# Two transformer blocks on one core: the memory's first key unit moved in front of the first MLP

## The reference, cut to what matters

```
x  = x + gate1 * (merged @ w_out)
h2 = rmsnorm(x, g_norm2) * (1 + scale2) + shift2
x  = x + gate2 * (square(relu(h2 @ w_mlp1)) @ w_mlp2)
x  = rmsnorm(x, g_final)
...
mem_n = rmsnorm(mem, mem_norm)                # over the 1024 features
h  = rmsnorm(x, norm_mix[0])
proj = h @ a_w_in[0]                          # gates, conv input, qm
kv = mem_n @ w_mem_kv[0]                      # k: columns 0:256, v: columns 256:512
k  = rmsnorm(k per head of 64, k_gain)        # the key's own norm
q  = rmsnorm(qm per head of 64, q_gain)
o  = softmax(q k^T / 8) v
```

## Time and profile before

| | |
|---|---|
| time, median of 3 runs | 1140.02 us (1136.89 to 1140.96) |
| the profiled execution's own time | 1139.74 us |
| its span | 1138.0 us, granted clock 0.971 |
| TensorE busy | 1080.2 us (95%) |
| TensorE weight loads busy | 1056.5 us (93%) |
| DVE, ACT, POOL busy | 645.0, 546.0, 370.6 us |
| DMA | 197.39 MB, mean 173 GB/s |
| chain that ended last | PE 77%, DVE 8%, ACT 6%, DMA 3% |

### The profile page before, as it was taken

How to read it: one execution, slowest core, us unless ns; L and a number is a source line. 1 busy time by engine, 2 the same in 40 slices (tenths; PEclk the granted TensorE clock), 3 DMA queues, 4 the chain that set the end, 5 groups by cost and what they waited for, 6 DMA issues and landing times.

```text
span 1138.0 us, 19842 instructions
## 1 busy us (share of the span) xinstructions
PE 1080.2 (95%) x8566; PEld 1056.5 (93%) x8566; DVE 645.0 (57%) x834; ACT 546.0 (48%) x770; POOL 370.6 (33%) x198
## 2 busy tenths in 40 slices
PE   6889999999899999999999999999999879999998
PEld 6889899899899999998999999999988769999998
DVE  3867657556676554544855544445866546544443
ACT  3366655653465544462344454443744534453441
POOL 2437148232275532442021252222522111252221
PEclk9999889999899999998999999999998889999999
DMA  9978357444458655534355555556533115555541
GB/s 325 288 252 258 117 182 241 165 150 149 148 192 276 202 183 186 185 112 148 112 177 188 191 185 183 181 182 203 161 115 108 42 37 178 196 184 183 186 149 38
DMA packets 173956, 197.39 MB, mean 173 GB/s; under 512 B 5379, under 2 KB 146092, under 8 KB 173740
## 3 DMA queue, kind: packets, MB, share of 16 engines
q1 hardware_dynamic: 173868, 196.11, 53.2%
HBM read 195.03 MB, written 1.06 MB: 172 GB/s over the span
## 4 chain that ended last, share of the span: by engine, by line
PE 77%; DVE 8%; ACT 6%; DMA 3%; issue 2%; POOL 2%; SPq 2%; DVEq 0%; ACTq 0%; POOLq 0%
PE bank L501 76%; DMA ada_raw<-in_w_ada 2%; DVE w_lo L1661 2%; ACT w_hi L1108 2%; ACT ada_raw L1098 2%; SPq L457 1%; ACT probs L1171 1%; POOL ada_raw L1511 1%; DMA probsT<-in_buckets 1%; DVE y_tok L1793 0%; POOL head_bias L1546 0%; DVE big L1892 0%; DVE probs L1768 0%; DVE idx L1865 0%; DVE big L2065 0%
## 5 line engine op out<-in xcount | busy, mean ns | idle before, releaser
L1661 DVE TENSOR_TENSOR w_lo<-w_raw,w_hi 128x2048 fp32r<-128x2048 f32 x158 | 387.3, 2454 | 258.0 <-ACT w_hi L1108 256.8
L501 PE MATMUL bank<-h_hi,w_hi 128*128 128x256 f32 x1328 | 381.2, 292 | 11.8 <-DVE w_lo L1661 7.5
L501 PE MATMUL bank<-h_hi,w_lo 128*128 128x256 f32 x1328 | 376.3, 289 | 0.0
L1108 ACT ACTIVATE w_hi<-w_raw 128x2048 fp32r<-128x2048 f32 x158 | 301.0, 1906 | 132.3 <-PE bank L501 124.6
L501 PE MATMUL bank<-h_lo,w_hi 128*128 128x256 f32 x1328 | 350.0, 286 | 0.6 <-POOL h_lo L1479 0.6
L501 PE MATMUL bank<-u_hi,w_hi 128*128 128x256 f32 x1024 | 287.6, 285 | 4.2 <-ACT u_hi L1117 2.3
L501 PE MATMUL bank<-u_hi,w_lo 128*128 128x256 f32 x1024 | 286.5, 284 | 0.0
L1479 POOL TENSOR_TENSOR u_lo<-fresh,u_hi 128x512 fp32r<-128x512 f32 x60 | 142.3, 2374 | 417.5 <-ACT u_hi L1117 417.4
L501 PEld LDWEIGHTS bank<-h_hi,w_hi 128*128 128x128 f32 x1328 | 263.3, 198 | 15.0 <-DVE w_lo L1661 9.4
L501 PE MATMUL bank<-u_lo,w_hi 128*128 128x256 f32 x1024 | 275.5, 284 | 0.0
L501 PEld LDWEIGHTS bank<-h_hi,w_lo 128*128 128x128 f32 x1328 | 262.7, 198 | 0.0
(11 more groups left out here) (245 smaller groups left out, 1035.9 us busy)
## 6 DMA issues: line engine op xcount, KB each, us to landing
w_raw<-in_w_mlp SPq DMA_DIRECT2D x32, 1024.0 KB, 5.4
w_raw<-in_w_up SPq DMA_DIRECT2D x32, 1024.0 KB, 5.5
w_raw<-in_w_down SPq DMA_DIRECT2D x32, 1024.0 KB, 5.0
w_raw<-in_w_in SPq DMA_DIRECT2D x21, 1024.0 KB, 5.3
ada_raw<-in_w_ada SPq DMA_DIRECT2D x19, 1024.0 KB, 7.8
w_raw<-in_a_w_in SPq DMA_DIRECT2D x10, 1024.0 KB, 5.1
w_raw<-in_w_o SPq DMA_DIRECT2D x8, 1024.0 KB, 5.0
w_raw<-in_w_out SPq DMA_DIRECT2D x4, 1024.0 KB, 5.0
```

The costliest lines, as they stand in the source:

```text
L501: return pe.matmul(dst, lhsT, rhs, start=start, stop=stop, skip_group_check=True)
L1108: act.activation(w_hi[:, n % PARTS_RING, :], w_raw[:, slot_of[n], :], ACT.Copy).then_inc(hi_w, 1)
L1661: dve.tensor_tensor(w_lo[:, n % PARTS_RING, :], w_raw[:, slot_of[n], :], w_hi[:, n % PARTS_RING, :].bitcast(F32), ALU.subtract).then_inc(l ...
```

## The change: what it does

The key unit of the memory's first attention becomes unit 30, in front of the first MLP; the MLP's units become 31 to 62, and the value unit stays behind them as unit 63. The key is now made from memory times the norm's weight, without the root of the memory's norm: ACT writes the high part to `u_hi` and DVE the low part to `u_lo`, pair by pair between the four residuals. TensorE runs the unit in two halves (`half_of`, by output columns), one behind the last product of `w_out` and one behind the last sums of squares. DVE takes the mean ahead of two splits of weights, where one split stood ahead of the mean. ACT evacuates the key there, into `mem_k0`, and squares it. Later, the memory's mean also gives `mem_eps`, EPS times the mean, and the key's own norm adds that in place of EPS, in two instructions in place of one. The value unit uses the normed memory as before.

```diff
@@ plan_units @@
-    mlp("mlp0", w["w_mlp1"], w["w_mlp2"])
     mem_unit(0, "k", 0)
+    mlp("mlp0", w["w_mlp1"], w["w_mlp2"])
     mem_unit(0, "v", MEM_W)
...
-N_... N_OUT, N_MLP0, N_M0 = ... 26, 30, 62
+N_... N_OUT, N_M0K, N_MLP0, N_M0V = ... 26, 30, 31, 63
...
@@ TensorE @@
             product(N_OUT + 3, h_hi, h_lo)
+
+            def half_of(n, nt, hi, lo):
+                if nt == 0:
+                    start_unit(n)
+                wh, wl = (t[:, n % PARTS_RING, :].rearrange("p (k n) -> p k n", k=KT) for t in (w_hi, w_lo))
+                for kt in range(KT):
+                    for i, (w, x) in enumerate(((wh, hi), (wh, lo), (wl, hi))):
+                        last = mm(lin[lin_bank[n]][:, nt * T:nt * T + T], w[:, kt, nt * P:nt * P + P], x[:, kt, :],
+                                  nt == 0 and kt == 0 and i == 0, kt == KT - 1 and i == 2)
+                if nt:
+                    last.then_inc(unit_done, 1)
+
+            pe.wait_ge(m0_lo, 4)
+            half_of(N_M0K, 0, u_hi, u_lo)
             add_squares(2, 2)
             add_squares(2, 3)
-            pe.wait_ge(fresh_ready, J_H2)
+            half_of(N_M0K, 1, u_hi, u_lo)
             spread_sum(2, ps_ada)
...
-            product(N_M0, mem_hi, mem_lo)
-            product_tok(N_M0 + 1, mem_hi, mem_lo)
+            product_tok(N_M0V, mem_hi, mem_lo)
@@ ScalarE @@
             for i in range(4):
                 split_w(N_OUT + i + AHEAD)
+                for k in (2 * i, 2 * i + 1):
+                    last = act.activation(u_hi[:, k, :], mem_pair[i][:, (k % 2) * T:(k % 2) * T + T], ACT.Copy,
+                                          scale=vec[:, V_MEM + k:V_MEM + k + 1])
+                last.then_inc(m0_hi, 1)
                 act.wait_ge(xt_ready, i + 1)
                 square_pair(2, i, flat(xT, 2 * i, 2 * i + 2))
+            split_w(N_M0K + AHEAD)
+            evac_qk("mem0", N_M0K, flat(mem_k0, 0, 2), mem_squares)
...
-            split_w(N_QM0)
+            split_w(N_QM0 + 1)
             squares_x("sum3")
-            evac_qk("mem0", N_M0, flat(mem_k[:, 0], 0, 2), mem_squares)
-            split_w(N_QM0 + 1)
             squares_x("sum3g")
-            evac(N_M0 + 1, flat(mem_v[:, 0], 0, 2))
+            evac(N_M0V, flat(mem_v[:, 0], 0, 2))
@@ VectorE @@
                 dve.drain().then_inc(xt_ready, 1)
+                dve.wait_ge(m0_hi, i + 1)
+                for k in (2 * i, 2 * i + 1):
+                    last = dve.scalar_tensor_tensor(out=u_lo[:, k, :], in0=mem_pair[i][:, (k % 2) * T:(k % 2) * T + T],
+                                                    scalar=vec[:, V_MEM + k:V_MEM + k + 1], in1=u_hi[:, k, :].bitcast(F32),
+                                                    op0=ALU.mult, op1=ALU.subtract)
+                last.then_inc(m0_lo, 1)
+            mean_square("sum2")
             split_w(N_OUT + 3 + AHEAD)
-            mean_square("sum2")
+            split_w(N_M0K + AHEAD)
             dve.wait_ge(spread_full, spread_no["sum2"] + 1)
             normed(J_H2, gs[:, 1, :], ps_ada, ada[:, 24:32])
...
+            def mean_mem():
+                from_misc("summem")
+                at = root_at["summem"]
+                link(dve.tensor_scalar(root[:, at:at + 2], ps_misc[:, 0:2], 1.0 / D, EPS, ALU.mult, ALU.add))
+                dve.tensor_scalar(mem_eps, root[:, at:at + 2], EPS, None, ALU.mult).then_inc(misc_read, 1)
...
-            mean_square("qk.mem0")
+            mean_square("qk.mem0", mem_eps)
```

More of the change, by code:

```diff
@@ L54 @@
 ADA_PE, ADA_DVE, ADA_POOL = (0, 3, 6), (1, 4, 7), (2, 5, *range(ADA_FIRST, ADA_UNITS))
-ADA_LATE = {**{2 + 2 * i: ADA_FIRST + i for i in range(12)}, **{32 + 4 * i: 20 + i for i in range(4)}}
+ADA_LATE = {**{2 + 2 * i: ADA_FIRST + i for i in range(12)}, **{33 + 4 * i: 20 + i for i in range(4)}}
 LOAD_LAG, COLUMNS_LAG = 2, 3
@@ L117, in plan_units @@
         n_unit("out", w["w_out"], 256 * i, "v")
+    mem_unit(0, "k", 0)
     mlp("mlp0", w["w_mlp1"], w["w_mlp2"])
-    mem_unit(0, "k", 0)
     mem_unit(0, "v", MEM_W)
@@ L147, in plan_units @@
     return units
-N_IDX, N_FOX, N_GF, N_DSA, N_GD, N_BR, N_OUT, N_MLP0, N_M0 = 0, 2, 8, 12, 18, 22, 26, 30, 62
+N_IDX, N_FOX, N_GF, N_DSA, N_GD, N_BR, N_OUT, N_M0K, N_MLP0, N_M0V = 0, 2, 8, 12, 18, 22, 26, 30, 31, 63
 N_QM0, N_CONV, N_O0, N_M1K, N_MLP1, N_M1V, N_QM1, N_O1, N_MLP2 = 64, 65, 74, 78, 79, 111, 117, 122, 126
@@ L325, in two_blocks @@
         mem_squares = flat(big, 12, 14)
+        mem_k0 = qk[:, 0:2, :]
+        mem_eps = stat[:, 86:88]
         x_hat = qk
@@ L353, in two_blocks @@
             "mem_sq", "mem_summed", "mem_normed", "mem_hi_done", "mem_lo_done"))
+        m0_hi, m0_lo = sem("m0_hi"), sem("m0_lo")
         consts_in, vec_in, x_in, small_in = (sem(s) for s in ("consts_in", "vec_in", "x_in", "small_in"))
@@ L882, in _ @@
             product(N_CONV + 1, h_hi, h_lo)
-            qk_squares("mem0", N_M0, mem_squares)
+            qk_squares("mem0", N_M0K, mem_squares)
             pe.wait_ge(root_ready, power_no["sum3"] + 1)
@@ L901, in _ @@
             pe.wait_ge(qk_normed, k_no["qk.mem0"] + 1)
-            attention("mem0.", 2, lambda g: qi[:, g, :], lambda g: mem_k[:, 0, g, :],
+            attention("mem0.", 2, lambda g: qi[:, g, :], lambda g: mem_k0[:, g, :],
                       lambda h, s: mem_v[:, 0, s, h * HD:h * HD + HD], FULL_BLOCKS, FULL_SPAN,
@@ L1274, in _ @@
                 split_h(J_MERGED + q, h_hi, 2 * q)
+            for half in range(2):
+                act.wait_ge(mem_in[half], 16)
+            act.wait_ge(unit_done, N_BR + 4)
             for i in range(4):
                 split_w(N_OUT + i + AHEAD)
+                for k in (2 * i, 2 * i + 1):
+                    last = act.activation(u_hi[:, k, :], mem_pair[i][:, (k % 2) * T:(k % 2) * T + T], ACT.Copy,
+                                          scale=vec[:, V_MEM + k:V_MEM + k + 1])
+                last.then_inc(m0_hi, 1)
                 act.wait_ge(xt_ready, i + 1)
                 square_pair(2, i, flat(xT, 2 * i, 2 * i + 2))
+            split_w(N_M0K + AHEAD)
+            evac_qk("mem0", N_M0K, flat(mem_k0, 0, 2), mem_squares)
             for q in range(4):
@@ L2012, in normed_mem @@
                 dve.drain().then_inc(misc_read, 1)
-            mlp(N_MLP0, ada[:, 40:48], {6: lambda: mean_square("summem"), 7: normed_mem})
+            mlp(N_MLP0, ada[:, 40:48], {6: mean_mem, 7: normed_mem})
             for q in range(4):
                 split_x(X_H4 + q, q, h_hi, h_lo, V_MIX)
-            split_w(N_QM0)
             split_w(N_QM0 + 1)
@@ L2039, in _ @@
                 last.then_inc(xt_ready, 1)
-            qk_scale("mem0", flat(mem_k[:, 0], 0, 2), V_MK, acc[1])
+            qk_scale("mem0", flat(mem_k0, 0, 2), V_MK, acc[1])
             split_w(N_CONV + 2 + AHEAD)
```

## The result

The changed kernel takes 1147.20 us (median of 7 runs, 1144.83 to 1149.83), the kernel before in the same comparison 1140.02 us (7 runs, 1136.89 to 1145.06). The ratio is 1.0069 with an interval of 1.0047 to 1.0092: slower, by 0.7%. The forecast was 1146.5 us, within 1140.5 to 1150.

What follows compares the result with a forecast made beforehand. TensorE, busy 1080.2 of 1138.0 us, was taken as the bound. Terms 6.0 + 1.4 - 2.8 + 2.0 + 0.2 = +6.8 us on the profiled 1139.74 gave 1146.5 us, range 1140.5 to 1150.

Steps and rivals of the forecast that it cites:

- the clock behind the MLP's start: First MLP's start: the 2.1 us low-clock loss stays because the empty stretch before it stays; 0, bounds -2.1 and +0.9.
- The wait for the low part: Before half 0 of mem0.k: TensorE idles 2.1 us, until 290.3, for the fourth pair's low part; within the +6.0.
- Mean and splits: Before the first MLP: DVE idles for the mean, then mean and two splits take 4.7 us; MLP starts 6.0 later.
- rival D: Before the first MLP: both splits shut out POOL's root, not one; +8.9, 1148.6 us; chance 0.10.
- first place: Second norm before the first MLP, where mem0.k is moved: MLP starts 6.0 us later, plus 1.4 for the clock.
- The clock in the first place: Behind the 2.1 us idle before half 0, the clock falls low for 3.4 us: +1.4.
- rival C: Clock stays 1.00 behind both idles, into the MLP and behind it: +1.3, 1141.0 us, no change; chance 0.15.
- the forecast's best case of -1.7: Splits out of the way, clock held, second place as forecast: 3.2 - 2.1 - 2.8 = -1.7 us.
- Second place: Behind the first MLP, without mem0.k: second unit waits for ACT's copy of mem0.v; -2.8, idle 4.1 us.
- The clock behind it: Behind the 4.1 us idle after the MLP, the clock falls low: +2.0, between 1.5 and 2.6.
- Rest: Key's norm: its mean takes two instructions instead of one, ahead of a split TensorE waits for: +0.2; other parts 0.
- B: Before half 0: the 2.1 us idle does not pull the clock down; +5.4, 1145.1 us; chance 0.20.

Runs made afterwards that it cites:

- e7: Kernel before plus only ACT's eight copies and DVE's eight low parts of memory, read by nobody, mem0.k unmoved: 1141.93 us, ratio 1.0026.
- e2: Changed kernel with half 0 of mem0.k waiting for the low parts pair by pair instead of for all four: 1146.79 us, ratio 1.0054.
- e8: Kernel before with only the mean of sum2 put ahead of DVE's split of unit 31: 1138.97 us, ratio 1.0002.
- e1: Changed kernel with DVE's two splits of weights ahead of the mean of sum2 instead of behind it: 1144.19 us, ratio 1.0043.
- e4: Changed kernel with the edits of e1, e2 and e3 together: 1136.75 us, ratio 0.9983.
- e3: Changed kernel with ACT's copy of mem0.v out of its bank ahead of the eight squares of sum3g: 1143.52 us, ratio 1.0031.
- e6: Changed kernel with 30 matmuls, read by nobody, in TensorE's idle ahead of the second unit behind the MLP: 1146.08 us, ratio 1.0062.
- e10: Changed kernel with the edits of e1, e2 and e3 together, measured again on another chip: 1137.09 us, ratio 0.9991.
- the three edits: Edits of e1, e2 and e3 together in the changed kernel, run as e4 and e10: 1136.75 and 1137.09 us.
- e9: Kernel before with only ACT's copy of mem0.v put ahead of the eight squares of sum3g: 1137.43 us, ratio 1.0000.
- e5: Changed kernel unaltered, measured again on a second chip against the kernel before: 1148.27 us, ratio 1.0081.

## Why the prediction was right

It was right by its mechanism, and each term of the sum can be set beside what the profile shows. One term that was put at nothing, the clock behind the MLP's start, was at nothing for another reason than the one given.

**The wait for the low part.** Forecast an idle of 2.1 us until 290.3; measured 1.98, until 290.52, ended by DVE's `u_lo`. e7 shows the low part's cost alone (0.8 us), and e2 that the idle goes when the half doesn't wait for all four.

**Mean and splits.** Forecast DVE idle for 5 us, then 4.7 us of work ahead of the normed pairs; measured 6.38 idle (the clock's 1.5 us included, which I had as a term of its own) and 4.6. Root and spread were forecast to end just ahead of the splits. They did: root at 299.77, 0.6 behind the first split's end at 299.2, where I had taken 0.9, and the spread at 300.5. DVE went on at 301.32 when its splits were through. So it was one split that held the root and not two; rival D did not come. The whole first place, clock and all, was forecast 7.4 us longer and is 7.25 longer.

Here a rule had spoken for more. The Trainium skill, page "SBUF — State Buffer", section "Who interferes with whom", lets whichever of the two issues first keep the shared port. For the root the runs agree: 2.69 us under a split (after, e8), 0.71 beside none (e1, e4). For the opposite direction the row is against it: with the root waiting beside them, the two splits took 4.49 us, the same as with POOL idle in e1. The 0.7 us that the rule would have added is not there. Beside larger work of POOL a split is held, though. Inside the MLP, in the changed kernel:

```profile
324.12 5.71 POOL L1534 TENSOR_TENSOR ada_raw<-ada_raw 128x1024 f32<-128x1024 f32 x2
324.63 4.06 DVE L1684 TENSOR_TENSOR w_lo<-w_raw,w_hi 128x2048 fp32r<-128x2048 f32 x1 [2.50 <-ACT w_hi L1124]
```

POOL was first there, and the split took 4.06 us instead of 2.29. How large POOL's operation has to be was not tried.

**The clock in the first place.** Forecast 1.4; half 0 took 294.96 - 290.52 = 4.44 us against 2.88, so 1.56 lost, of which the sum took 1.4.

**The clock behind the MLP's start.** The forecast read 2.1 us of loss there and took it as unchanged. The term of 0 came out: the MLP was as long as before to 0.1 us (from its first matmul to the memory's unit 189.22 us before and 189.17 after). But the reading of 2.1 us was wrong, for this low stretch costs next to nothing. In e3 the clock was 1.00 there:

```profile
302.60:306.00 3.40, 3.17 (x24) 2.99 (x25) 3.33 (x5) 0.63 (x1) 2.25 (x2) 1.00 1.10 362
```

Its MLP took 189.27 us all the same. The reason is that TensorE isn't what sets the pace there. The normed pairs come 2.43 us apart from DVE (302.75, 305.19 and 307.62 after), and TensorE at full clock waits for each (0.20 to 0.27 us in e3). Then comes the held split shown above. The matmul behind it starts 25.2 us behind the MLP's start in each case: 328.84 - 303.65 after, with the clock low for 3.4 us, 327.81 - 302.62 in e3 with none low, and 321.45 - 296.21 before with 4.9 us low. After and in e3 it has an idle of 0.43 us in front; before there is none, the slower matmuls fill it. So the -2.1 us of rival C, and the same 2.1 in the forecast's best case of -1.7, could not be had.

**Second place.** Forecast -2.8, with an idle of 4.1 us ended by ACT's `mem_v`; measured 199.94 - 202.76 = -2.82, idle 3.89, the releaser as named: ACT's eight squares from 499.68 still stand ahead of the copy. e3 shows the cause: with the copy first the idle falls to 0.70 us and 3.1 us come back.

**The clock behind it.** Forecast +2.0 between 1.5 and 2.6; measured 13.93 - 11.59 = +2.34, and e6 (filled idle: 11.58) shows that it is the idle's price. The price is not fixed: behind the same idle both units took 13.9 and 14.0 us in the two profiles of this kernel, 13.1 in e2 and 12.8 in e1, so 1.2 to 2.4 us.

**Rest.** Forecast +0.2 for the two-instruction mean ahead of the split; from the mean of the norm to TensorE's next unit it was 2.60 us instead of 2.42, +0.18.

At that point, 532.35 us after against 525.40 before, the two profiles are 6.95 us apart; the forecast had 6.8. (Of the 6.95, 0.19 lay ahead of the first mark, and a low stretch just ahead of this point cost 0.2 less than before; the two cancel.) What the profile loses beyond is no term of the sum: behind the short idle there (0.85 us, 0.67 before) the clock was low for 3.4 us, which costs 1.5, and another 1.6 came by 941 us. The stretch of 4.5 us at this same mark in the kernel after, the kernel before, e7 and e10, in this order:

```profile
532.40:536.90 4.50, 4.50 (x25) 4.50 (x26) 4.50 (x9) 0.00 (x0) 3.85 (x2) 0.62 0.79 251
```

```profile
525.40:529.90 4.50, 4.50 (x37) 4.50 (x38) 4.50 (x9) 0.00 (x0) 3.90 (x2) 1.00 0.75 252
```

```profile
526.10:530.60 4.50, 4.50 (x25) 4.50 (x26) 4.50 (x9) 0.00 (x0) 3.83 (x2) 0.62 0.80 256
```

```profile
523.00:527.50 4.50, 4.50 (x37) 4.50 (x38) 4.50 (x9) 0.00 (x0) 3.90 (x2) 1.00 0.75 250
```

25 matmuls or 37 in the same time. The clock was low in e7, which has the short idle of the kernel before (0.67) and no moved unit, and at 1.00 in e10, which has the long one (0.86). So neither the moved unit nor the longer idle decides it alone. Over all twelve profiles it was low in seven of the eight with the moved unit and in two of the four without. Whether the moved unit makes it more frequent is open, and so is how much of the 7.2 and 10.4 us between the medians comes from such stretches.

**The rivals.** B, that the first idle leaves the clock up, was wrong in both profiles of this kernel and right in the one of e3, at the same idle. C needed a clock of 1.00 behind both idles. It did not come here. Half of its mechanism exists: in e1, e3, e4 and e10 the clock is 1.00 from half 1 into the MLP. But it is worth nothing there, as said. Of the chances, slower adds up to 0.59 from the forecast's own shares, where it has 0.55. The forecast also held that with the splits out of the way, the clock held and the second place as it is, -1.7 us was the best to be had. e4 goes by another way, with the waits gone too: first place 10.40 - 7.83 = +2.6, MLP to second unit 196.8 - 202.8 = -6.0, so -3.4 by the marks, and -2 by the medians.

What stays open: whether the kernel with the three edits is faster than the kernel before (two intervals that reach 1.0003 and 1.0008); whether the moved unit is then worth anything, for e9 without it has the same median within 0.3 us, and only the marks put the three edits ahead, by some 2.2 us (3.4 against 1.1); and what decides if the clock falls behind an idle of given length.

## What to carry to other kernels

Work that is moved into a gap must have its own inputs ready when the gap opens, and must not stand in front of what the gap was waiting for. Here 5.76 us of matmuls were put into a place where TensorE idled for 4.73 of 8.00 us, and they made the way 7.25 us longer; with waits by piece and DVE's splits ahead of the mean again, the same matmuls cost 2.6. When work leaves a place, look at which engine's queue sets the next release there: 5.76 us were taken from TensorE and 2.8 were gained, until ACT's copy was put ahead of squares that are used only behind both units. An idle of TensorE is priced with the low clock that may follow, here 1.5 us on top of 2.0, and 1.2 to 2.4 on top of 3.9. And a low clock is priced only where TensorE sets the pace: behind the MLP's start 3.4 to 4.9 us of it cost nothing that lasted.

## What the runs showed that I had not expected

The same idle at the same place does not always bring the clock down. Behind 1.98 us ahead of half 0 it was low in four profiles (the changed kernel, e1, e5, e6) and 1.00 in e3; behind 0.67 us at the later mark it was 1.00 in the kernel before and low in e7. Behind 3.9 us it was low in all four profiles that had it, and behind the 2.97 us of the earlier trace rows in all twelve. The Trainium skill, page "TensorE: Matmul & The Clock Gate", section "What's actually happening", says that the chip looks at activity on a schedule of its own, which doesn't start with the kernel. These rows agree with that, and it would account for much of the spread of single runs: the 29 runs of the kernel before on one chip go from 1134.8 to 1142.9 us with the same code. That it does was not shown.

A local mark is therefore worth more than a total. Edits of 0.9 to 3.6 us (e2, e8, e9) were read to 0.1 us between two marks, and the totals of 9 to 12 runs could not size them.
